# Transposing x by column tiles inside the output product, and multiplying the first two up tiles together

## What is computed

```python
def _merge(conv_o, attn_o, lp):
    o = _rmsnorm(attn_o, lp['g_o']).reshape(B, T, D_ATTN)
    return jnp.dot(jnp.concatenate([conv_o, o], axis=-1), lp['w_out'])

def _ffn(u_hist, lp):
    uc = _dwconv_valid(u_hist, lp['w_dw_f'], lp['b_dw_f'])
    gate, val = jnp.split(uc, 2, axis=-1)
    return jnp.dot(jax.nn.silu(gate) * val, lp['w_down'])
...
    x1 = x + gt1 * _merge(conv_o, o, lp)
    h2 = _rmsnorm(x1, lp['norm2']) * (1 + sc2) + sh2
    u = jnp.dot(h2, lp['w_up'])
...
    y = x1 + gt2 * _ffn(u_hist, lp)
```

## Time and profile before

| | |
|---|---|
| time, median of 3 runs | 3149.05 us (3143.93 to 3151.16) |
| the profiled execution's own time | 3160.05 us |
| its span, first to last instruction | 3158.1 us |
| PE busy | 2958.3 us, 94% of the span |
| DVE, POOL, ACT busy | 1310.2, 1248.4, 917.1 us |
| mean granted PE clock | 0.961 |

### The profile page before, as it was taken

How to read it: one execution, slowest core, us unless ns; L and a number is a source line. 1 busy time by engine, 2 the same in 40 slices (tenths; PEclk the granted TensorE clock), 3 DMA queues, 4 the chain that set the end, 5 groups by cost and what they waited for, 6 DMA issues and landing times.

```text
span 3158.1 us, 55457 instructions
## 1 busy us (share of the span) xinstructions
PE 2958.3 (94%) x21496; PEld 2704.1 (86%) x21500; DVE 1310.2 (41%) x2660; ACT 917.1 (29%) x1690; POOL 1248.4 (40%) x1694
## 2 busy tenths in 40 slices
PE   6698899999989769997999999999999999999998
PEld 3197478889955549996999999999999999999998
DVE  1424359999867451006232323233232323232322
ACT  1212323332125331123323232323232323222332
POOL 0044254453320243432444444444444444444442
PEclk9899899999989889996999999999999999999999
DMA  8822256552268663221222322222222232322223
GB/s 249 284 75 62 61 165 184 165 164 58 79 210 281 216 200 94 73 75 47 81 88 81 88 81 84 85 82 87 82 87 82 82 87 81 88 81 84 86 83 93
DMA packets 448284, 356.57 MB, mean 113 GB/s; under 512 B 27785, under 2 KB 391973, under 8 KB 446885
## 3 DMA queue, kind: packets, MB, share of 16 engines
q1 hardware_dynamic: 437282, 327.85, 34.7%
q0 software_dynamic: 8704, 19.27, 1.9%
q10 hardware_dynamic: 2075, 6.34, 0.7%
HBM read 346.15 MB, written 7.96 MB: 112 GB/s over the span
## 4 chain that ended last, share of the span: by engine, by line
PE 70%; issue 14%; DVE 10%; POOL 4%; DMA 1%; ACT 1%; POOLq 0%; SPq 0%; ACTq 0%; DVEq 0%
PE ps L1160 62%; POOL wlo L703 4%; DVE ye L1984 2%; DVE yb L1981 2%; PE ps L1194 1%; DMA raw<-in_w_ada 1%; DVE prod L1965 1%; DVE scP L1892 1%; PE ps L1326 1%; PE ps L1572 1%; PE ps L1370 1%; PE ps L1514 1%; PE ps L1529 1%; DVE yb L1968 0%; DVE scP L1921 0%
## 5 line engine op out<-in xcount | busy, mean ns | idle before, releaser
L703 POOL TENSOR_TENSOR wlo<-raw,whi 128x256 fp32r<-128x256 f32 x1480 | 1135.7, 799 | 1623.8 <-ACT whi L776 1623.8
L1160 PE MATMUL ps<-XH,whi 128*128 128x288 f32 (+1 forms) x4512 | 987.4, 300 | 41.4 <-POOL wlo L703 22.1
L1160 PE MATMUL ps<-XH,wlo 128*128 128x288 f32 (+1 forms) x4512 | 975.1, 297 | 0.0
L1160 PE MATMUL ps<-XL,whi 128*128 128x288 f32 (+1 forms) x4512 | 967.9, 296 | 0.0
L776 ACT ACTIVATE whi<-raw 128x1024 fp32r<-128x1024 f32 x370 | 390.8, 1057 | 1688.2 <-PE ps L1160 1537.1
L1160 PEld LDWEIGHTS ps<-XH,whi 128*128 128x128 f32 (+1 forms) x4512 | 731.5, 190 | 66.5 <-issue 26.2
L1160 PEld LDWEIGHTS ps<-XL,whi 128*128 128x128 f32 (+1 forms) x4512 | 731.1, 190 | 0.0
L1160 PEld LDWEIGHTS ps<-XH,wlo 128*128 128x128 f32 (+1 forms) x4512 | 728.4, 190 | 0.0
L2219 DVE SCALAR_TENSOR_TENSOR tmp<-up,vT,tmp 128x512 f32<-128x512 f32 x88 | 98.6, 1120 | 740.9 <-ACT tmp L1058 738.5
L1160 PE MATMUL ps<-gH,whi 128*128 128x288 f32 x1408 | 301.6, 295 | 2.5 <-ACT us L1051 2.0
L1160 PE MATMUL ps<-gH,wlo 128*128 128x288 f32 x1408 | 302.5, 296 | 0.0
(11 more groups left out here) (303 smaller groups left out, 2428.7 us busy)
## 6 DMA issues: line engine op xcount, KB each, us to landing
raw<-in_w_ada SPq DMA_DIRECT2D x192, 512.0 KB, 4.8
raw<-in_w_up SPq DMA_DIRECT2D x176, 512.0 KB, 3.9
raw<-in_w_down SPq DMA_DIRECT2D x88, 512.0 KB, 3.6
raw<-in_w_in SPq DMA_DIRECT2D x72, 512.0 KB, 5.1
Vp<-in_cache_v POOLq DMA_DIRECT2D x128, 128.0 KB, 3.9
raw<-in_w_out SPq DMA_DIRECT2D x32, 512.0 KB, 4.0
raw<-in_cache_k SPq DMA_DIRECT2D x64, 128.0 KB, 2.4
xN<-in_x_prompt ACTq DMA_DIRECT2D x4, 1024.0 KB, 11.5
```

The source lines that it names most:

```text
L703: last = G.tensor_tensor(wlo[:, u.slot(m, 2), a:a + width // 4], raw[:, u.slot(m, 4), a:a + width // 4], whi[:, u.slot(m, 2), a:a + width ...
L1160: ins = mm(dst[:, t, :], wt, x(k0 + k, t), start=st, stop=sp_)
```

## The change

In the output product, x is no longer loaded by whole rows and transposed ahead of the product. SP loads it by columns, one tile of 128 columns for all tokens at a time (`x_columns`, two buffers `xC`), and PE makes its five transposes between the two units of that tile's product (`x_rows`), into banks 4 and 5. VectorE copies the row into `x1T` (`x_row`) ahead of the tile's residual. ScalarE rounds the first two weight units of the product before the last root of the decode, and the rows of `convT` no longer wait for `s_doe`; VectorE puts `d_out` between its second and third subtraction.

After the product, the last two sums and the root come ahead of the state's transposes. The four units of the first two up tiles (gate and value) are loaded and split together, two of them into spare buffers `whB` and `wlB` (`parts`), and PE multiplies both tiles k tile by k tile. The norm work of a k tile is spread over three engines and four buffers (`norm_in`): VectorE multiplies by `rstd` and subtracts XL two k tiles later, ScalarE scales and shifts the 512 prompt columns and rounds into XH, GpSimd scales and shifts the 64 sampled columns. GpSimd does this between the low parts of unit 3 and unit 4.

Context lines are left out.

```diff
@@ -293,7 +293,7 @@
-        xN2 = at(o_tab, "xN2", [128, 2, D])
+        xC = at(o_tab + 5632, "xC", [128, 2, 5, 128])
@@ -307,7 +307,10 @@
-        sN = at(o_tab, "sN", [128, SN_T * 128])
+        sN = at(o_c, "sN", [128, SN_T * 128])
+        o_b = o_c + SN_T * 512
+        whB = at(o_b, "whB", [128, 2, 1024], F32R)
+        wlB = at(o_b + 8192, "wlB", [128, 2, 1024], F32R)
@@ -383,7 +386,7 @@
-        s_mh = sem("s_mh")
+        s_mh, s_nm, s_nt = sem("s_mh"), sem("s_nm"), sem("s_nt")
@@ -405,6 +408,15 @@
+        def norm_in(k):
+            return (tmp, sq)[k % 4 // 2][:, k % 2, :]
...
+        def parts(u, m):
...
+            if u.base == U_FFN and u.per == 0 and m in (2, 3):
+                return whB[:, m - 2], wlB[:, m - 2]
+            return whi[:, u.slot(m, 2)], wlo[:, u.slot(m, 2)]
@@ -616,16 +628,23 @@
+            def x_columns(n, slot):
...
+                sp.dma_start(xC[:, slot, 0:4, :], x_prompt[0].rearrange("(t p) d -> p t d", p=128)[:, :, bass.ds(n * 128, 128)])\
+                    .then_inc(s_x2[slot], 16)
+                sp.dma_start(xC[0:NS, slot, 4, :], x_sample.rearrange("b t d -> (b t) d")[:, bass.ds(n * 128, 128)])\
+                    .then_inc(s_x2[slot], 16)
...
-            sp.wait_ge(s_doe, DQ)
-            for n in range(5):
-                w(sp, s_x2t, 4 * (n - 1))
-                src = x_prompt[0, n * 128:n * 128 + 128, :] if n < 4 else x_sample.rearrange("b t d -> (b t) d")
-                sp.dma_start(xN2[0:128 if n < 4 else NS, n % 2, :], src).then_inc(s_x2[n % 2], 16)
+            sp.wait_ge(s_dv, 4 * DQ)
+            for c in range(2):
+                x_columns(c, c)
...
+                    sp.wait_ge(s_x2t, 2 * i + (c - 1))
+                    x_columns(2 * i + c, c)
@@ -655,7 +674,10 @@
-            for j in range(GT):
+            for m in range(4):
+                taken(Tally(U_FFN).index(m) - 4)
+                half(Tally(U_FFN), m, m // 2, wup, m % 2 * DFF)
+            for j in range(1, GT):
@@ -698,10 +720,11 @@
+                    h, l = parts(u, m)
...
-                        last = G.tensor_tensor(wlo[:, u.slot(m, 2), a:a + width // 4], raw[:, u.slot(m, 4), a:a + width // 4],
-                                               whi[:, u.slot(m, 2), a:a + width // 4].bitcast(F32), ALU.subtract)
+                        last = G.tensor_tensor(l[:, a:a + width // 4], raw[:, u.slot(m, 4), a:a + width // 4],
+                                               h[:, a:a + width // 4].bitcast(F32), ALU.subtract)
@@ -733,7 +756,16 @@
-            with pool.Fori(0, 2) as i:
+            lo(Tally(U_FFN), 0, 4)
...
+            for k in range(KT):
+                t = by8(norm_in(k)[:, SEQ:T])
+                pool.wait_ge(s_ht, KT + k + 1)
+                G.tensor_tensor(t, t, modA[:, k, 1:].unsqueeze(2).to_broadcast([128, DB, DS]), ALU.mult).then_inc(s_nm, 1)
+                pool.wait_ge(s_nm, 2 * k + 1)
+                G.tensor_tensor(t, t, adaT[:, 48 + k, 1:].unsqueeze(2).to_broadcast([128, DB, DS]), ALU.add).then_inc(s_nm, 1)
+            lo(Tally(U_FFN), 4, 4)
+            with pool.Fori(1, 2) as i:
@@ -769,11 +801,11 @@
-            def hi(u, k, n=1, width=1024):
+            def hi(u, k, n=1, width=1024, spare=False):
...
-                    act.wait_ge(s_used, u.index(m) + 1)
-                    A.activation(whi[:, u.slot(m, 2), 0:width], raw[:, u.slot(m, 4), 0:width], ACT.Copy)\
+                    act.wait_ge(s_sne if spare else s_used, 1 if spare else u.index(m) + 1)
+                    A.activation(parts(u, m)[0][:, 0:width], raw[:, u.slot(m, 4), 0:width], ACT.Copy)\
@@ -1006,14 +1038,17 @@
+                else:
+                    hi(Tally(U_OUT), 0, 2)
...
-            act.wait_ge(s_doe, DQ)
...
+                if k == 8:
+                    act.wait_ge(s_doe, DQ)
...
-            hi(Tally(U_OUT), 0, 4)
+            hi(Tally(U_OUT), 2, 2)
@@ -1024,6 +1059,12 @@
+            square_x1(KT - 2, 0)
+            square_x1(KT - 1, 1)
+            hi(Tally(U_FFN), 0)
+            act.wait_ge(s_ssq, 2 * KT)
+            A.activation(halves(rstd[:, :]), pair(6), ACT.Sqrt, bias=eps[:, 0:1], scale=1.0 / D).then_inc(s_sqr, 1)
+            hi(Tally(U_FFN), 1)
@@ -1032,12 +1073,15 @@
-            square_x1(KT - 2, 0)
-            square_x1(KT - 1, 1)
-            act.wait_ge(s_ssq, 2 * KT)
-            A.activation(halves(rstd[:, :]), pair(6), ACT.Sqrt, bias=eps[:, 0:1], scale=1.0 / D).then_inc(s_sqr, 1)
-            hi(Tally(U_FFN), 0, 2)
-            operand_hi(1)
+            hi(Tally(U_FFN), 2, 2, spare=True)
+            for k in range(KT):
+                t = norm_in(k)
+                act.wait_ge(s_ht, KT + k + 1)
+                A.activation(t[:, 0:SEQ], t[:, 0:SEQ], ACT.Identity, bias=adaT[:, 48 + k, 0:1], scale=modA[:, k, 0:1])\
+                    .then_inc(s_nt, 1)
+                act.wait_ge(s_nm, 2 * k + 2)
+                act.wait_ge(s_nt, k + 1)
+                A.activation(XH[:, k, :], t, ACT.Copy).then_inc(s_hh, 1)
@@ -1085,10 +1129,8 @@
-                else:
-                    hi(u, 2)
-                hi(u, 4 * j + 3)
-                up_evac(u, 4 * j + 1, 0, j, 0)
+                    hi(u, 4 * j + 3)
+                up_evac(u, 4 * j + (1 if j else 2), 0, j, 0)
@@ -1147,12 +1189,12 @@
-                s = u.slot(m, 2)
+                hp, lp = parts(u, m)
...
-                    h, l = whi[:, s, a:a + width], wlo[:, s, a:a + width]
+                    h, l = hp[:, a:a + width], lp[:, a:a + width]
@@ -1646,24 +1688,24 @@
-            for n in range(20):
-                tt, q = n // 4, n % 4
-                r = 128 if tt < 4 else NS
-                pe.wait_ge(s_x2[tt % 2], 16 * (tt // 2 + 1))
-                w(pe, s_x2e, n - 3)
-                for j in range(4):
-                    c = (4 * q + j) * 128
-                    ins = tr(bank(4 + n % 4, 128, j * 128, j * 128 + r), xN2[0:r, tt % 2, c:c + 128], ident[0:r, 0:r])
-                ins.then_inc(s_x2t, 1)
-            gemm(Tally(U_OUT), 0, 0, operand_from=KT)
-            gemm(Tally(U_OUT), 2, 1)
-            pe.wait_ge(s_x2e, 20)
+            def x_rows(i, c):
...
+                pe.wait_ge(s_x2[c], i * 32 + 32)
+                if c or not isinstance(i, int) or i:
+                    pe.wait_ge(s_x2e, 2 * i + c)
+                for t in range(4):
+                    tr(bank(4, 128, t * 128, t * 128 + 128), xC[:, c, t, :], ident)
+                tr(bank(5, 128, 0, NS), xC[0:NS, c, 4, :], ident[0:NS, 0:NS]).then_inc(s_x2t, 1)
...
+            pe.wait_ge(s_doe, DQ)
+            gemm(Tally(U_OUT), 0, 0, operand_from=KT, middle=lambda: x_rows(0, 0))
+            gemm(Tally(U_OUT), 2, 1, middle=lambda: x_rows(0, 1))
...
-                    gemm(Tally(U_OUT, i, 4), 2 * c, c)
+                    gemm(Tally(U_OUT, i, 4), 2 * c, c, middle=lambda: x_rows(i, c))
@@ -1675,15 +1717,16 @@
+            sum_x1(KT - 2, 0)
+            sum_x1(KT - 1, 1)
...
+            pe.wait_ge(s_x1, KT)
...
-            sum_x1(KT - 2, 0)
-            sum_x1(KT - 1, 1)
@@ -1726,8 +1769,15 @@
-            for j in range(GT):
-                up_gemm(Tally(U_FFN), 4 * j, 0, j, 0, operand_from=2 * KT if j == 0 else None)
+            u = Tally(U_FFN)
+            for h in range(2):
+                pe.wait_ge(s_lo, u.index(2 * h + 1) + 1)
+                for k in range(8):
+                    for v in range(2):
+                        unit(u, 2 * h + v, pair(2 * v), 8 * h, h == 0, h == 1 and k == 7, kts=k + 1, k_from=k, opH=XHt, opL=XLt,
+                             inc=k == 7, operand_from=2 * KT)
+            for j in range(1, GT):
+                up_gemm(Tally(U_FFN), 4 * j, 0, j, 0)
@@ -2167,17 +2217,20 @@
-            d_out(DQ - 1)
...
+                if k == 2:
+                    d_out(DQ - 1)
...
-            for n in range(20):
-                x_in(n, 4 + n % 4, s_x2t, s_x2e, x1T)
-            dve.wait_ge(s_x2e, 20)
...
+            def x_row(n):
+                row = x1T[:, bass.ds(n, 1), :].rearrange("p a t -> p (a t)")
+                dve.wait_ge(s_x2t, n + 1)
+                V.tensor_copy(row[:, 0:SEQ], bank(4))
+                V.tensor_copy(row[:, SEQ:T], bank(5, 128, 0, NS)).then_inc(s_x2e, 1)
+                dve.wait_ge(s_x2e, n + 1)
@@ -2194,6 +2247,7 @@
+                    x_row(2 * i + c)
@@ -2201,11 +2255,16 @@
-            operand(1, 48, False)
+            for k in range(KT + 2):
+                if k < KT:
+                    TT(norm_in(k), x1T[:, k, :], rstd[:, :], ALU.mult).then_inc(s_ht, 1)
+                if k >= 2:
+                    dve.wait_ge(s_hh, KT + k - 1)
+                    TT(XL[:, k - 2, :], norm_in(k - 2), XH[:, k - 2, :].bitcast(F32), ALU.subtract).then_inc(s_X, 1)
+                    dve.wait_ge(s_X, 2 * KT + k - 1)
...
-            dve.wait_ge(s_x2e, 20)
```

## The result

The kernel after the change takes 3120.09 us (median of 4 runs, 3113.89 to 3125.8), the kernel before beside it 3148.41 (4 runs): 28.3 us less by the medians, a ratio of 0.9906 with a 95% interval of 0.9888 to 0.9925. Forecast were 3125, 23.7 less, in a range of 3111 to 3140. The profiled execution of after took 3120.35, its span is 3118.7.

A forecast was written before the change was run, and what follows sets the result against it. PE was taken as full in most slices, so time is won only where it stands still or runs at half clock. Terms -12.8 (product) and -10.9 (up tiles) sum to -23.7 off the median 3149.05: 3125, range 3111 to 3140.

The forecast's parts named there:

- Product starts 24.0 sooner: Start of the output product: without the x transposes ahead of it, PE is let go at 1169.7, 24.0 us earlier.
- the rival with 5%: Output product's start: early weight rounding does not pass, low weights come late, 11.7 us gained instead of 24.0; 3137, 5%.
- A break at 0.7, 11.2 in all: Inside the output product: five transposes with switch cost 0.7 in each of 16 column tiles, 11.2 us; bounds 10.4 to 15.5.
- First up matmul at E+19.5, behind GpSimd: First up tiles: PE starts 19.5 us after the last output matmul ends, held by GpSimd's four low parts and norm share.
- 0.34 for a 64-column GpSimd operation: GpSimd's norm share: 0.34 us per 64-column operation, from a line through 256 and 160 columns; bounds 0.2 and 0.53.
- Pace 2.24 by exclusion: First two up tiles: VectorE and GpSimd exclude each other, so 1.55+0.69=2.24 us a k tile.
- the rival without exclusion: First two up tiles: GpSimd slips into VectorE's gaps, PE's 1.59 paces, tiles end at 46.9 after the product; 3118, 25%.
- the sum: Whole change: the main case, -12.8 at the product and -10.9 at the up tiles, 23.7 us less; 40%.
- Up tiles at 1.6 a k tile: First two up tiles: a pace of 1.6 us a k tile, listed as a sign that the prediction is wrong.
- Third tile 5.8 later and at half clock: Third up tile: PE starts 5.8 us after the first two tiles end and loses about 2.0 to the slow start.
- The rivals at 3137 and 3138: Up tiles: GpSimd starved by VectorE (3137, 10%) or half clock throughout (3138, 15%); product: weights late (3137, 5%).
- The side of slower: Output product: each of 16 breaks brings back the half-clock start (2.0), product 32 us longer, +8.3 in all; 3157, 5%.

The follow-up runs named there:

- the wide operation: Kernel after the change with GpSimd's second operation per k tile 256 columns wide instead of 64, norm's shift left out; pace 2.00 a k tile, tiles 3.4 us longer.
- The product's part alone: Kernel after the change with only its output-product part, norm and first up tiles as before the change; ratio to before 0.9959 (0.9945 to 0.9974).

## Why the prediction was right, and where its steps were not

The time fell well inside the range, and most steps went as forecast. That it came within 5 us of the figure is partly luck, since two steps missed in opposite directions.

1. *Product starts 24.0 sooner*: right, 24.2, for the reasons given. The early `hi` passed, GpSimd had both parts by 1155.9, and PE was let go by `d_out`. No wait for weights or x appeared (the rival with 5%).
2. *A break at 0.7, 11.2 in all*: mis-sized. It is 0.84 by the rows, so 13.4, and 13.75 in all between the profiled products; the rest is the half clock at the start, which lasted 4.5 us in place of 3.9. That is inside the bounds of 10.4 to 15.5. The step that failed is to take "the lower side": the four large transposes kept the 0.13 each (1168.81 to 1169.33), but the small fifth took 0.21 to the next start and the pair behind it lost 0.11. The part gave 24.2-13.75=10.5, not 12.8.
3. *First up matmul at E+19.5, behind GpSimd*: right in the mechanism, and forecast 1.5 too late. GpSimd was at its four parts from E+3.2 to E+15.8, 12.6 in place of 13.7: the three products of VectorE held it up by 1.5 (7.07 for eight pieces in place of 5.52) and not by 2.3, and undisturbed parts took 11.0, not 11.4.
4. *0.34 for a 64-column GpSimd operation*: the line through its two rows gives 0.35; it took 0.29 alone.
5. *Pace 2.24 by exclusion*: wrong, the step that carries the miss. It added GpSimd's 0.69 to VectorE's 1.55. The exclusion exists, as the wide operation shows (pace 2.00) and as the earlier trace rows had shown with pieces of 256 columns, but what VectorE loses goes by GpSimd's columns. Two operations of 64 cost it 0.1 a k tile (0.86 in place of 0.76 once), and PE's 1.59 paces, as the rival without exclusion had it (25%): both tiles done at E+45.7, for E+46.9 there and E+54.7 in the sum. The rows at hand showed the loss beside pieces of 256 columns (0.52); the prediction took from them that there is one, and sized it by the narrow operation's whole duration. "Up tiles at 1.6 a k tile" stood among its signs of being wrong, and occurred.
6. *Third tile 5.8 later and at half clock*: right, 5.70 ended by GpSimd's low part, and 2.6 for the slow start where 2.0 was forecast. It is as good as E+54.0 then, 19.4 less than before, where the sum had 10.9.

The Trainium skill, SBUF — State Buffer, section "SBUF: two separate sides", by which the sum was taken, calls the lock held for a whole instruction. The trace agrees that GpSimd is held off for as long as VectorE's instruction lasts (0.71 to 0.81 for 0.29), and differs on what GpSimd's instructions cost VectorE: by that rule an estimate of twice 0.29, 0.58 a k tile; measured 0.1. Here the measurement decides.

So the total came out 5 lower than forecast, by two misses of opposite sign, 8.5 more gained at the up tiles and 2.3 less at the product; what is left of the difference is scatter. The rivals at 3137 and 3138 didn't occur: the clock rose after 4 us and GpSimd was never starved in that stream. The side of slower, breaks that cost the clock, was tried with breaks twice as long and didn't occur either.

## What to carry to other kernels

Price contention between two engines by the part of an instruction that moves columns, from rows of at least two widths, and not by its whole duration. Here a 64-column operation between the other engine's instructions was nearly free, up to one for each of them. When two tiles are made to end together, look at who prepares the third: here the gap that this opened cost 7.7 us, more than the 3.3 that the interleaving gained, and two calls moved ahead took it away. A wait that ends on the slowest queue, as GpSimd's four parts ahead of its first small operation did, is shortened by handing that queue less ahead of it, even to an engine that is itself in the stream.

## What the runs showed of the hardware

GpSimd and VectorE, both with two SBUF inputs: a 64-column GpSimd operation takes 0.29 alone and 0.71 to 0.81 beside a stream of VectorE, one for each VectorE instruction. Behind it VectorE's subtraction goes from 0.76 to 0.86, behind one of 256 columns to 1.29.

The clock of PE at the start of a stretch isn't a function of the gap alone. Behind gaps of 2.02 and 2.03 the same code started once at full and once at half clock, in one execution each. The product that begins 1.8 behind the last transpose was at half clock from its first pair in two traces (that of after is one). In the others it began at full clock and fell to half within 1 us, so that its length is 0.5 to 0.8 shorter. The product's part alone shows it:

```profile
1168.72 0.53 PE L1170 MATMUL ps<-XH,whi 128*128 128x288 f32 x2 [1.45 <-DVE qT L2164]
...
1169.72 0.69 PE L1170 MATMUL ps<-XH,whi 128*128 128x288 f32 x2
```

With the tiles one by one PE waited 0.5 in each of four k tiles of 1.57 and kept a granted clock of 1.00 (1413.2 to 1421), while before it ran at 0.50 for 42 us with waits of 0.63 in every 2.43.
